# The last stage of a decoder block: the residual add of five of eight output tiles moved from VectorE to GpSimd, with four accumulators and the final scaling three tiles late

## The reference, cut to what matters

```
    out = jax.ops.segment_sum(ys * buf_w[:, None], buf_tok, num_segments=m + 1)[:m]
...
        x = x + gt2 * hierarchical_moe(h, w_group[l], b_group[l], w_expert[l], b_expert[l], w1[l], w3[l], w2[l])
    return rmsnorm(x, normf_g)
```

## Time and profile before

| | us |
|---|---|
| median of three runs | 2002.7 (2001.5 to 2002.86) |
| the profiled execution's own time | 1999.94 |
| its span in the profile | 1998.2 |
| time outside the span (1999.94 - 1998.2) | 1.74 |
| TensorE busy in the span | 1938.0 (97%) |
| VectorE busy | 1344.8 (67%) |
| GpSimd busy | 222.5 (11%) |
| first multiplication of the tail (L2867) starts at | 1954.97 |

### The profile page before, as it was taken

One profiled execution on the slowest core, in us unless ns is written; L12 is line 12 of the kernel. 1 busy time (PEld: TensorE's weight loads), 2 busy tenths in 40 slices (PEclk: granted clock), 3 DMA queues, 4 the chain that ended last, 5 costly groups with the idle time before them and its releaser, 6 DMA issues.

```text
span 1998.2 us, 28045 instructions
## 1 busy us (share of the span) xinstructions
PE 1938.0 (97%) x9687; PEld 1613.2 (81%) x9687; DVE 1344.8 (67%) x1786; ACT 941.5 (47%) x1279; POOL 222.5 (11%) x179
## 2 busy tenths in 40 slices
PE   6999999999999999999999899997999999999996
PEld 5788888888888888888888777886888888888883
DVE  6545453111658568577585556567999999999996
ACT  5211111111444525535445243214788887878863
POOL 0000000000111021021110100001222122222210
PEclk7999999999999999999999999997999999999998
DMA  8242423211323222232231669437999999999966
GB/s 312 67 130 74 147 73 102 81 63 63 101 71 86 72 72 81 67 98 69 71 86 61 208 221 295 140 104 290 372 377 381 381 381 386 384 384 382 401 257 257
DMA packets 220504, 382.11 MB, mean 191 GB/s; under 512 B 49909, under 2 KB 162982, under 8 KB 194982
## 3 DMA queue, kind: packets, MB, share of 16 engines
q1 hardware_dynamic: 202566, 333.89, 47.9%
q10 hardware_dynamic: 8672, 30.76, 4.0%
q0 software_dynamic: 9216, 16.80, 2.2%
HBM read 348.50 MB, written 49.67 MB: 199 GB/s over the span
## 4 chain that ended last, share of the span: by engine, by line
PE 73%; DVE 12%; DMA 6%; issue 4%; ACT 3%; SPq 1%; DVEq 0%; ACTq 0%; POOLq 0%
PE ps L710 33%; PE ps L2774 17%; PE ps L2818 8%; PE ps L2669 4%; PE ps L2760 1%; DVE vv L1706 1%; DVE qk L1706 1%; DMA inv_rows<-inv_d 1%; DMA inv_d<-sub_x 1%; DVE LX L1883 1%; DVE pair_prod L1781 1%; PE ps L2573 1%; PE ps L2603 1%; PE ps L2798 1%; PE ps L2617 1%
## 5 line engine op out<-in xcount | busy, mean ns | idle before, releaser
L605 DVE TENSOR_TENSOR mw_lo<-mw_raw,mw_hi 128x2048 fp32r<-128x2048 f32 x192 | 436.7, 2289 | 44.3 <-ACT mw_hi L600 44.0
L710 PE MATMUL ps<-h_hi,w_lo 128*128 128x512 f32 x1152 | 462.0, 401 | 0.5 <-DVE h_lo L1571 0.5
L710 PE MATMUL ps<-h_hi,w_hi 128*128 128x512 f32 x1152 | 449.2, 390 | 0.0
L710 PE MATMUL ps<-h_lo,w_hi 128*128 128x512 f32 x1152 | 448.7, 389 | 0.0
L600 ACT ACTIVATE mw_hi<-mw_raw 128x2048 fp32r<-128x2048 f32 x192 | 368.1, 1919 | 116.2 <-PE ps L2774 67.0
L710 PEld LDWEIGHTS ps<-h_hi,w_hi 128*128 128x128 f32 x1152 | 216.2, 188 | 45.8
L710 PEld LDWEIGHTS ps<-h_hi,w_lo 128*128 128x128 f32 x1152 | 216.8, 188 | 40.8 <-DVE h_lo L1571 0.6
L710 PEld LDWEIGHTS ps<-h_lo,w_hi 128*128 128x128 f32 x1152 | 216.8, 188 | 39.3
L671 DVE TENSOR_TENSOR w_lo<-w_raw,w_hi 128x1024 fp32r<-128x1024 f32 x88 | 107.6, 1223 | 155.4 <-ACT w_hi L666 154.2
L2774 PE MATMUL ps<-mw_hi,xT_lo 128*128 128x512 f32 x512 | 204.1, 399 | 3.0 <-DVE xT_lo L2206 2.3
L2774 PE MATMUL ps<-mw_hi,xT_hi 128*128 128x512 f32 x512 | 201.1, 393 | 0.0
(11 more groups left out here) (402 smaller groups left out, 3072.1 us busy)
## 6 DMA issues: line engine op xcount, KB each, us to landing
mw_raw<-in_w_dram SPq DMA_DIRECT2D x192, 1024.0 KB, 8.4
w_raw<-in_w_in_dram SPq DMA_DIRECT2D x72, 512.0 KB, 4.1
ada_b<-in_w_ada_dram SPq DMA_DIRECT2D x8, 2048.0 KB, 7.9
y_t<-y_d SPq DMA_DIRECT2D x7, 1024.0 KB, 10.1
ada_sc<-in_w_ada_dram SPq DMA_DIRECT2D x4, 1024.0 KB, 8.7
w_raw<-in_w_proj_b_dram SPq DMA_DIRECT2D x8, 512.0 KB, 4.2
merged_b_d<-sc_y ACTq DMA_DIRECT2D x8, 512.0 KB, 2.6
decay<-crow_d SPq DMA_DIRECT2D x8, 512.0 KB, 5.9
```

The costliest lines, as they stand in the source:

```text
L605: dve.tensor_tensor(mw_lo[off % NSPLIT][:], mw_raw[off % NRAW][:], mw_hi[off % NSPLIT][:], ALU.subtract).then_inc(mw_lo_done, 1)
L710: last = pe.matmul(dst, lhs[:, s, k], rhs[:, k, cols], start=(k == 0 and part == 0), stop=(k == KD - 1 and part == 2))
```

## The change

The tail gets four accumulators in place of two (tile n uses n % 4). For the tiles 1 to 5 (`BY_POOL`) GpSimd adds `x1`, as soon as VectorE has weighed the tile; VectorE adds for the tiles 0, 6 and 7 alone. ScalarE's square of a tile waits for whoever adds it. VectorE's scalings stand three tiles behind its weighings: it weighs tiles 0, 1 and 2, then weighs tile n and scales tile n - 3 for n = 3 to 7, and at the end it scales tiles 5, 6 and 7. `weighed(n)` is the count of `acc_step` when tile n has been weighed. `res` has two buffers as before, ScalarE's order of square, root and store is the same, and the matrices, loads and stores are the same.

```diff
-    y_acc = at("y_acc", [P, 2, D])
+    y_acc = at("y_acc", [P, 4, D])
+    BY_POOL = range(1, 6)
...
+        def weighed(n):
+
+            return 4 + n + max(0, n - len(BY_POOL) - 1)
...
+            for n in BY_POOL:
+                pool.wait_ge(acc_step, weighed(n))
+                pool.tensor_tensor(y_acc[:, n % 4], y_acc[:, n % 4], x1[:, n], ALU.add).then_inc(pool_step, 1)
...
             for n in range(TT):
-                act.wait_ge(acc_step, 2 * n + 4)
-                act.activation(y_sq[:], y_acc[:, n % 2], ACT.Square, accum_out=stat3[:, 0, n:n + 1])\
+                if n in BY_POOL:
+                    act.wait_ge(pool_step, 9 + len(LEVELS) + n)
+                else:
+                    act.wait_ge(acc_step, weighed(n) + (1 if n else 0))
+                act.activation(y_sq[:], y_acc[:, n % 4], ACT.Square, accum_out=stat3[:, 0, n:n + 1])\
...
-                    if n >= 2:
-                        dve.wait_ge(res_done, n - 1)
-                        dve.wait_ge(x1_squared, TT + n - 1)
...
-                        dve.wait_ge(acc_step, 2 * n + 3)
-                        dve.tensor_tensor(y_acc[:, s], y_acc[:, s], x1[:, n], ALU.add).then_inc(acc_step, 1)
...
+            def weigh(n):
+
+                s = n % 4
+                if n >= 4:
+                    dve.wait_ge(res_done, n - 3)
+                    dve.wait_ge(x1_squared, TT + n - 3)
...
+                if n not in BY_POOL:
+                    dve.wait_ge(acc_step, weighed(n))
+                    dve.tensor_tensor(y_acc[:, s], y_acc[:, s], x1[:, n], ALU.add).then_inc(acc_step, 1)
...
+            for n in range(3):
+                weigh(n)
+            for n in range(3, TT):
+                weigh(n)
+                finish(n - 3)
+            for m in range(TT - 3, TT):
+                finish(m)
...
-                    pe.wait_ge(acc_step, 2 * (n - 4) + 3)
+                    pe.wait_ge(acc_step, weighed(n - 4))
```

More of the change, by code:

```diff
@@ L2275, in _ @@
             dve.wait_ge(rows_in, 16 * 7)
-            for n in range(TT + 1):
-                if n < TT:
-                    s = n % 2
-                    if n >= 2:
-                        dve.wait_ge(res_done, n - 1)
-                        dve.wait_ge(x1_squared, TT + n - 1)
[L2283 to L2295, removed]
-                        dve.wait_ge(acc_step, 2 * n + 3)
-                        dve.tensor_tensor(y_acc[:, s], y_acc[:, s], x1[:, n], ALU.add).then_inc(acc_step, 1)
[L2298 to L2308, removed]
@@ new lines, in weigh @@
+            def weigh(n):
[3 more added lines that the diff above has]
+                    dve.wait_ge(x1_squared, TT + n - 3)
+                if n == 0:
+                    for half in range(2):
+                        cols = slice(half * HALF, (half + 1) * HALF)
+                        dve.wait_ge(y_summed, half + 1)
+                        dve.tensor_tensor(y_acc[:, 0, cols], ps[:, half], gt2_row[:, cols], ALU.mult)\
+                           .then_inc(acc_step, 1)
+                        dve.wait_ge(acc_step, 2 * half + 1)
+                        dve.tensor_tensor(y_acc[:, 0, cols], y_acc[:, 0, cols], x1[:, 0, cols], ALU.add)\
+                           .then_inc(acc_step, 1)
+                    return
+                dve.wait_ge(y_summed, n + 2)
+                dve.tensor_tensor(y_acc[:, s], ps[:, 2 * (n % 4):2 * (n % 4) + 2].rearrange("p b d -> p (b d)"),
+                                  gt2_row[:], ALU.mult).then_inc(acc_step, 1)
+                if n not in BY_POOL:
+                    dve.wait_ge(acc_step, weighed(n))
+                    dve.tensor_tensor(y_acc[:, s], y_acc[:, s], x1[:, n], ALU.add).then_inc(acc_step, 1)
@@ new lines, in finish @@
+            def finish(m):
+                dve.wait_ge(x1_root, TT + m + 1)
+                dve.reciprocal(stat3[:, 2, m:m + 1], stat3[:, 1, m:m + 1]).then_inc(x1_inv, 1)
+                dve.wait_ge(x1_inv, TT + m + 1)
+                if m >= 2:
+                    dve.wait_ge(res_out[m % 2], 16 * (m // 2))
+                for cols in (slice(0, D),) if m < TT - 1 else (slice(0, HALF), slice(HALF, D)):
+                    dve.scalar_tensor_tensor(out=res[:, m % 2, cols], in0=y_acc[:, m % 4, cols],
+                                             scalar=stat3[:, 2, m:m + 1], in1=nf_row[:, cols],
+                                             op0=ALU.mult, op1=ALU.mult).then_inc(res_done, 1)
```

## The result

The changed kernel is slower. Twenty runs of it gave a median of 2004.59 us (2003.14 to 2008.07), twenty of the kernel before, the first three among them, 2000.55 us (1997.12 to 2003.38). The ratio is 1.0022, with a 95% interval of 1.0015 to 1.0029: some 4.4 us, 3.0 to 5.8 (the medians alone differ by 4.0). The time lies inside the range, but only by the part that the range took over from a rival: the forecast case, VectorE first, ended at 2003.4. I had given the forecast of no measurable change 0.84; the rival "GpSimd first" is what happened. The interval reaches 1.4 us to each side, so a change of 3.6 us can be told from none; I had reckoned with 4.0.

The account below looks back on a forecast made before the run. VectorE was taken as the bound, 3.91 us a tile against TensorE's 3.43. Fewer adds, less deferred scalings and store waits, left 0.6 us gain: 2002.7 - 0.6 = 2002.1 us, range 2000.4 to 2006.8.

Parts of the forecast that it names:

- VectorE first: Behind weighings 3 to 5, VectorE's scaling gets the memory before GpSimd's add: 0.6 us gained, 2002.1 us, chance 0.57.
- no measurable change: Whole kernel: the time stays within about 0.2%, 4.0 us, of before; chance 0.84.
- GpSimd first: Rival: behind weighings 3 to 5, GpSimd's add holds each scaling about 2.4 us; 3.6 us slower, 2006.3 us, chance 0.28.
- What bounds the tail: Tail before the change: VectorE is the bound at 3.91 us a tile, against TensorE's 3.43.
- Part one: Tiles 1 to 5: five adds, 6.3 us, leave VectorE; TensorE becomes the bound, so only VectorE's backlog can be gained.
- part two: Behind tile 7: four scalings, not two; scalings 6 and 7 wait for stores 4 and 5, leaving 0.56 us gain.
- Part three: GpSimd's adds beside VectorE: one engine waits for the other's whole instruction; scalings can be held, weighings are free.
- Which one: Race of GpSimd's add and VectorE's scaling behind weighings 3 to 5: GpSimd's lead of 0.02 to 0.04 us not enough.
- the mask row: Earlier trace: GpSimd's mask started 0.07 us before VectorE's 16-element add, which took 0.18; weak evidence for VectorE getting in first.
- What would show it: Signs in the changed profile: scalings 0 to 2, adds 3 to 5, and scalings 6 and 7 waiting 1.2 and 0.5 us.

Follow-up runs that it names:

- e1: Changed kernel, with GpSimd's add of tiles 3, 4 and 5 also waiting for VectorE's scaling of the tile three before; stretch 33.96 us, ratio 1.0005.
- e3: Changed kernel, with the reciprocal of tile n - 3 moved ahead of the weighing of tile n; stretch 33.22 us, ratio 0.9994.
- e9: Changed kernel, with three tiny GpSimd writes between GpSimd's wait and each of its adds; stretch 33.61 us, ratio 0.9995.
- e2: Changed kernel, with no tile given to GpSimd and all adds on VectorE; stretch 34.95 us, ratio 1.0006.
- e4: e1 with eight result buffers and ScalarE's squares of tiles 6 and 7 ahead of the late stores; stretch 32.61 us, ratio 0.9997.
- e10: No decoder block: VectorE and GpSimd operations raced, 0 to 64 tiny VectorE writes shifting starts; the scaling took 1.28 us when 0.06 ahead.

## Why the prediction was wrong, point by point

- **What bounds the tail.** Right: VectorE at 3.91 us a tile, TensorE at 3.43. In e1 and e3, with the holds gone, the weighings of tiles 2 to 6 stand 3.43 to 3.53 apart.
- **Part one and part two, the backlog and the stores.** The mechanism was right and the size nearly: 33.6 was the sum, e9 gave 33.61, e3 33.22, e1 33.96. Scaling 6 waited for store 4 and scaling 7 for store 5, each 2.6 us from issue to landing. e2 and e4 set the prices of its two sides apart: the order alone costs 0.8, stores and squares 1.35.
- **Part three, the hold.** Right in kind and price: one engine waits for the other's whole instruction, weighings are free. The rival was priced at +3.6 and came to +3.27; the add took 2.34, not 2.39, and weighing 6 began 4.0 late, at 1988.22 against 1967.07 + 5 x 3.43 = 1984.22, where I had 4.15.
- **Which one, the step that failed.** I wrote that the mask row showed VectorE first though GpSimd had started 0.07 before, since VectorE's add "took 0.18, not the 0.34 that waiting for the mask's end at 2.66 would make". The 0.34 is the wait, 0.16, plus the add's whole length. But a held operation is under way already while it waits: the earlier trace rows had shown it, and I had used it for the scaling (1.1 after the add, not 1.28) and not here. What is left of a 16-element add when it is let go is 0.02, as e10 shows, and 2.66 + 0.02 is 2.68 = 2.50 + 0.18. The row that I took as evidence for VectorE showed it being held. "GpSimd seems to ask for the memory some 0.1 us after its record's start" had no other support, and it gave such a delay to GpSimd alone. In e10 the scaling has to start 0.03 to 0.05 us ahead to get in first; the prediction let it come 0.02 to 0.04 behind.
- With that row read rightly, everything spoke for GpSimd, whose record starts 0.02 to 0.04 ahead, and the sum would have been 2006.3. That sum stood on 2002.7, the median of three runs; on 2000.55, the median of twenty, the same 3.6 us give 2004.2, against 2004.59 measured. The Trainium skill's page "SBUF — State Buffer", section "SBUF: two separate sides", has the rule that whoever starts first has the shared ports for the whole instruction. The traces here agree with it, by the records' starts to within 0.05 us: a scaling less than 0.03 us ahead still comes second.
- **What would show it.** The list held: scalings at 3.4 beside adds at 2.34 was the sign of "GpSimd first". Scaling 6 waited 0.53 for its root and 0.66 more for store 4, 1.2 together as I had it; scaling 7 waited 0.22 for store 5, where I had 0.5.

Why GpSimd starts 0.02 ahead: its start lags the weighing's end by 0.08 (1975.24 - 1975.16), and the scaling, behind a reciprocal, by 0.10. That is shown. Open is one hold that is longer than all this gives: in the earlier trace rows the product that starts at 547.06, with 0.29 us of a GpSimd spread left to run, took 2.09, 0.86 more than its 1.23, with the next spread close behind. No run here took up short GpSimd operations in a row.

## What to carry to other kernels

Before work is given to GpSimd, list which VectorE operations will run beside it and read two SBUF tiles: each can be held for a whole GpSimd instruction, and it will not show as idle but as a longer operation. Two tiles are not the whole test: the operation held in the earlier trace rows, 1.10 for 0.487, reads one SBUF tile and a column of factors, while the reciprocal of a single column kept its 0.15 inside GpSimd's add in e1 (at 1978.98). So look for each kind of operation in a trace. Where both are released by the same event, do not leave the order to hundredths of a microsecond; let the one with slack wait for the other, or start the urgent one sooner. And when a pipeline is loosened, give buffers to what the bound engine's own waits name (here the results, 2.36 us), not to what the new order wants.

## What the hardware showed that I had not expected

- The turn is sharp: VectorE 0.06 ahead keeps its 1.28 us and GpSimd's add takes 3.42; a dead heat gives 3.42 and 2.34. Whoever comes second ends a fixed time after the first one's end, the same to the hundredth in trial after trial of a pair: 1.08 for a scaling behind an add, and for an add behind a scaling 2.20 in e10 and 2.22 in e3 and e9.
- A held operation has done its start-up while it waits: what is left after release is 1.08 of 1.28 us for a scaling, 2.20 of 2.34 for GpSimd's add, and 0.02 of 0.16 for a 32x16 add. An estimate from these: the scaling wants the memory 0.20 us after its record's start, the two adds 0.14 after theirs. Then a scaling must start 0.06 ahead of GpSimd's add to be first, near the 0.03 to 0.05 measured, and the small add wins a dead heat, as it did (0.16 at 133.25 in e10). That this is how the order is made is not shown.
- Size is no shelter: a VectorE add of 16 elements took 2.35 us behind a GpSimd add that had started 0.02 before.
- Tiny writes ahead of an operation move its start by far less than their own length: one GpSimd write of 0.10 us moved the add from 0.08 behind the weighing's end to 0.11, VectorE's of 0.06 us moved the scaling by 0.01 to 0.02 each.
